# Low parts of 32 up-projection tiles made in the merge stage, stored and loaded back; dots moved out of the last stage

## The reference

```python
g_conv = jax.nn.sigmoid(g_conv + b_merge[:D_MODEL])
g_attn = jax.nn.sigmoid(g_attn + b_merge[D_MODEL:])
merged = g_conv * y_conv + g_attn * y_attn
return jnp.einsum("bsd,de->bse", merged, w_o)
...
e = (jnp.take_along_axis(i1, ci // P_TOPK, axis=-1) * N_KEYS
     + jnp.take_along_axis(i2, ci % P_TOPK, axis=-1))
g = jax.nn.softmax(vals, axis=-1)
...
a = jnp.einsum('cd,ckd->ck', xc, expert_u[ec])
w = (gc * jax.nn.gelu(a.astype(jnp.float32))).astype(x.dtype)
return jnp.einsum('ck,ckd->cd', w, expert_v[ec])
```

## Time and profile before

| | us |
|---|---|
| median of 3 runs | 2193.1 (2191.36 to 2194.11) |
| the profiled execution | 2191.2 |
| its span, first to last instruction | 2189.5 |
| TensorE busy | 2124.8 (97%) |
| VectorE busy | 1650.1 (75%) |
| ScalarE busy | 1042.0 (48%) |
| GpSimd busy | 638.7 (29%) |

### The profile page before, as it was taken

How to read it: one execution, slowest core, us unless ns; L and a number is a source line. 1 busy time by engine, 2 the same in 40 slices (tenths; PEclk the granted TensorE clock), 3 DMA queues, 4 the chain that set the end, 5 groups by cost and what they waited for, 6 DMA issues and landing times.

```text
span 2189.5 us, 33425 instructions
## 1 busy us (share of the span) xinstructions
PE 2124.8 (97%) x11713; PEld 1787.7 (82%) x11713; DVE 1650.1 (75%) x3228; ACT 1042.0 (48%) x1940; POOL 638.7 (29%) x425
## 2 busy tenths in 40 slices
PE   7999999999999988899999989999999999999999
PEld 6888888888888545687899988999998888888777
DVE  6555555534367687564399999999988989999999
ACT  5333333322243477744455535999844333343332
POOL 0000000000040000020100223777626767777773
PEclk9999999999999999999999999999999999999999
DMA  5322222232234200022355888999989999999997
GB/s 195 97 86 86 86 86 95 80 99 98 98 101 177 77 1 1 1 68 87 125 177 177 279 260 290 382 408 400 392 306 408 419 418 418 418 418 418 411 418 290
DMA packets 137228, 484.57 MB, mean 221 GB/s; under 512 B 15056, under 2 KB 30416, under 8 KB 135184
## 3 DMA queue, kind: packets, MB, share of 16 engines
q1 hardware_dynamic: 75456, 229.93, 30.0%
q0 software_dynamic: 59056, 225.14, 26.1%
q10 hardware_dynamic: 2592, 27.85, 3.1%
HBM read 435.42 MB, written 46.92 MB: 220 GB/s over the span
## 4 chain that ended last, share of the span: by engine, by line
PE 63%; DVE 21%; DMA 10%; ACT 3%; issue 2%; POOL 1%; ACTq 0%; DVEq 0%; POOLq 0%
PE bank L495 15%; PE bank L496 15%; PE bank L497 15%; DMA rows<-peer_v,idxU 9%; PE bank L1257 7%; DVE rows L2327 6%; DVE wlo L482 4%; PE bank L510 2%; DVE own L2332 2%; DVE hot L2485 2%; DVE hot L2483 2%; PE bank L610 1%; PE bank L570 1%; PE bank L813 1%; PE bank L1211 1%
## 5 line engine op out<-in xcount | busy, mean ns | idle before, releaser
L495 PE MATMUL bank<-act_hi,whi 128*128 128x320 f32 (+1 forms) x1840 | 646.4, 351 | 23.2 <-DVE wlo L482 19.8
L496 PE MATMUL bank<-act_lo,whi 128*128 128x320 f32 (+1 forms) x1840 | 635.1, 345 | 0.0
L497 PE MATMUL bank<-act_hi,wlo 128*128 128x320 f32 (+1 forms) x1840 | 634.8, 345 | 0.0
L482 DVE TENSOR_TENSOR wlo<-raw,whi 128x1024 fp32r<-128x1024 f32 x398 | 485.8, 1222 | 141.5 <-ACT whi L478 139.3
L478 ACT ACTIVATE whi<-raw 128x1024 fp32r<-128x1024 f32 x398 | 416.4, 1055 | 262.5 <-PE bank L1257 114.1
L495 PEld LDWEIGHTS bank<-act_hi,whi 128*128 128x128 f32 x1840 | 346.0, 188 | 65.7 <-DVE wlo L482 23.4
L497 PEld LDWEIGHTS bank<-act_hi,wlo 128*128 128x128 f32 x1840 | 345.8, 188 | 32.7
L496 PEld LDWEIGHTS bank<-act_lo,whi 128*128 128x128 f32 x1840 | 346.2, 188 | 31.4 <-issue 0.7
L762 POOL DMA_INDIRECT rows<-peer_u,idxU x128 | 196.7, 1537 | 337.5 <-DVE udot L2327 168.9
L1257 PE MATMUL bank<-whi,h_hi 128*128 128x512 f32 x768 | 238.4, 391 | 7.1 <-DVE wlo L482 4.2
L1257 PE MATMUL bank<-whi,h_lo 128*128 128x512 f32 x768 | 237.4, 390 | 0.0
(11 more groups left out here) (403 smaller groups left out, 2905.6 us busy)
## 6 DMA issues: line engine op xcount, KB each, us to landing
raw<-tiles SPq DMA_DIRECT2D x398, 512.0 KB, 4.9
gates_dram<-stage ACTq DMA_DIRECT2D x12, 2048.0 KB, 11.6
wg<-gates_dram POOLq DMA_DIRECT2D x16, 1536.0 KB, 17.0
acts_dram<-gelu SPq DMA_DIRECT2D x120, 160.0 KB, 5.1
hf<-acts_dram POOLq DMA_DIRECT2D x30, 640.0 KB, 13.6
bias<-alibi POOLq DMA_DIRECT2D x16, 256.0 KB, 2.9
w1s<-cmp_w POOLq DMA_DIRECT2D x1, 4096.0 KB, 13.0
res<-x_t ACTq DMA_DIRECT2D x4, 512.0 KB, 6.9
```

The costliest lines, as they stand in the source:

```text
L482: dve.tensor_tensor(wlo[:, j.slot, :], raw[:, j.slot, :], whi[:, j.slot, :].bitcast(F32), ALU.subtract).then_inc(lo_made, 1)
L495: pe.matmul(to, wh, x, start=(kc == 0), stop=False)
L496: pe.matmul(to, wh, xl, start=False, stop=False)
L497: last = pe.matmul(to, wl, x, start=False, stop=(kc == KC - 1))
```

## The change

Between the merge stage's pairs of jobs stand pairs of tiles of the up projection (jobs 36 to 67): they are loaded, rounded and split like every tile, but not multiplied; the low part is stored to a new DRAM tensor `lo_dram`. The merge stage so has 64 ring positions instead of 32, of which TensorE uses 32. VectorE hands the stored slots on (`low_stored`) when both stores of a pair have landed. In the up projection the same 32 tiles are loaded again (their high part is made again), and their low part is loaded from `lo_dram` by SyncE; VectorE only signals that it is there. The dots are redistributed: 12 for 6 in tile 2, 28 for 18 in tile 3, 72 for 76 in the gates stage, 18 for 12 in the rest, so that 62 instead of 80 stay for the last stage. Two semaphores are merged into one (`res_step`).

```diff
-J_C = J_B + 32
+J_C = J_B + 64
+EARLY_LO = range(36, 68)
-DOTS_TILE = [(0, 0), (0, 0), (6, 10), (18, 0)]
-DOTS_GATES = 76
-DOTS_REST = 12
+DOTS_TILE = [(0, 0), (0, 0), (12, 10), (28, 0)]
+DOTS_GATES = 72
+DOTS_REST = 18
@@ SyncE
+            with sp.Fori(0, J_C // RING - J_B // RING) as i:
+                for m in range(RING):
+                    load(Job(J_B + RING + m, i))
+                    if m >= 2:
+                        sp.dma_start(lo_dram[bass.ds(i * 2 + m - 2, 1), :, :],
+                                     wlo[:, m, :].bitcast(F32)).then_inc(S("lo_moved"), 16)
...
+            def store_and_load(i, at_, with_lo):
                 for m in range(RING):
-                    j = Job(J_U + m, i)
+                    j = Job(J_U + at_ + m, i)
                     was_taken(sp, j)
-                    sp.dma_start(acts_dram[bass.ds(i * RING + m, 1), :, :], gelu[:, m, :])\
+                    sp.dma_start(acts_dram[bass.ds(i * RING + at_ + m, 1), :, :], gelu[:, m, :])\
                         .then_inc(acts_stored[m], 16)
-                    load(Job(J_U + 8 + m, i))
+                    if with_lo:
+                        sp.wait_ge(S("lo_moved"), (i * RING + len(EARLY_LO) + m) * 16)
+                        sp.dma_start(wlo[:, j.slot, :].bitcast(F32), lo_dram[bass.ds(i * RING + m, 1), :, :])\
+                            .then_inc(S("lo_moved"), 16)
+                    load(Job(J_U + at_ + 8 + m, i))
+
+            first, end = EARLY_LO.start - RING, EARLY_LO.stop - RING
+            for low, high in ((0, first), (first, end), (end, U_REST)):
+                with sp.Fori(0, (high - low) // RING) as i:
+                    store_and_load(i, low, low == first)
@@ TensorE, merge stage
             with pe.Fori(0, 4) as i:
-                for m in range(8):
-                    ...
-                    multiply(pe, Job(J_B + m, i, 8), hi, lo)
+                for m in range(16):
+                    j = Job(J_B + m, i, 16)
+                    if m % 4 < 2:
+                        ...
+                        multiply(pe, j, hi, lo, after_stored(Job(J_B - 1 + m, i, 16)) if m % 4 == 0 else None)
@@ VectorE, merge stage
+                def low_stored(unit, *stored_jobs):
+                    dve.wait_ge(S("lo_moved"), (unit + 1) * 32)
+                    for j in stored_jobs:
+                        dve.wait_ge(taken[j.slot], j.turn + 1)
+                        dve.sem_inc(taken[j.slot], 1)
+                        dve.sem_inc(job_done, 1)
                 for h in range(2):
                     chunk = bass.ds(i * 2 + h, 1)
-                    make_lo(dve, J(4 * h).ahead())
-                    by_root(tg[:, :], J(4 * h), r_one[:, :])
-                    make_lo(dve, J(4 * h + 1).ahead())
+                    make_lo(dve, J(8 * h + 2))
+                    make_lo(dve, J(8 * h + 3))
+                    by_root(tg[:, :], J(8 * h), r_one[:, :])
+                    make_lo(dve, J(8 * h + 4))
                     dve.wait_ge(conv_tanh, i * 2 + h + (KC + 1))
-                    result_of(dve, J(4 * h + 1))
+                    result_of(dve, J(8 * h + 1))
                     dve.wait_ge(mg_split, i * 2 + h + 1)
                     dve.scalar_tensor_tensor(out=m1[:, :], in0=tg[:, :], scalar=1.0, in1=bank[1][:, :],
                                              op0=ALU.add, op1=ALU.mult).then_inc(taken[1], 1)
-                    make_lo(dve, J(4 * h + 2).ahead())
-                    was_taken(dve, J(4 * h + 1))
-                    by_root(tg[:, :], J(4 * h + 2), r_one[:, :])
-                    make_lo(dve, J(4 * h + 3).ahead())
+                    low_stored(i * 4 + 2 * h, J(8 * h + 2), J(8 * h + 3))
+                    make_lo(dve, J(8 * h + 5))
+                    was_taken(dve, J(8 * h + 1))
+                    make_lo(dve, J(8 * h + 6))
+                    make_lo(dve, J(8 * h + 7))
+                    by_root(tg[:, :], J(8 * h + 4), r_one[:, :])
+                    make_lo(dve, J(8 * h + 8))
                     dve.wait_ge(attn_tanh, i * 2 + h + (KC + 1))
...
+                    low_stored(i * 4 + 2 * h + 1, J(8 * h + 6), J(8 * h + 7))
+                    make_lo(dve, J(8 * h + 9))
+                    was_taken(dve, J(8 * h + 5))
@@ VectorE, up projection
             def u_job(n):
-                make_lo(dve, Job(J_U + n).ahead())
+                j = Job(J_U + n).ahead()
+                if n + AHEAD in EARLY_LO:
+                    dve.wait_ge(hi_made, j.n + 1)
+                    dve.wait_ge(S("lo_moved"), 16 * (len(EARLY_LO) + n + AHEAD - EARLY_LO.start + 1))
+                    dve.sem_inc(lo_made, 1)
+                else:
+                    make_lo(dve, j)
```

More of the change, by code:

```diff
@@ L656, in _ @@
                 load(Job(m))
-            with sp.Fori(1, (J_U + 8) // RING) as i:
+            with sp.Fori(1, J_B // RING + 1) as i:
                 for m in range(RING):
                     load(Job(m, i))
+            with sp.Fori(0, J_C // RING - J_B // RING) as i:
[4 more added lines that the diff above has]
+                                     wlo[:, m, :].bitcast(F32)).then_inc(S("lo_moved"), 16)
+            with sp.Fori(0, (J_U + 8) // RING - J_C // RING - 1) as i:
+                for m in range(RING):
+                    load(Job(J_C + RING + m, i))
             for m in range((J_U + 8) // RING * RING, J_U + 8):
                 load(Job(m))
-            with sp.Fori(0, U_REST // RING) as i:
+            def store_and_load(i, at_, with_lo):
                 for m in range(RING):
-                    j = Job(J_U + m, i)
+                    j = Job(J_U + at_ + m, i)
                     was_taken(sp, j)
-                    sp.dma_start(acts_dram[bass.ds(i * RING + m, 1), :, :], gelu[:, m, :])\
+                    sp.dma_start(acts_dram[bass.ds(i * RING + at_ + m, 1), :, :], gelu[:, m, :])\
                         .then_inc(acts_stored[m], 16)
-                    load(Job(J_U + 8 + m, i))
+                    if with_lo:
[7 more added lines that the diff above has]
+                    store_and_load(i, low, low == first)
             with sp.Fori(0, (JOBS - J_U - U_REST - 8) // RING) as i:
@@ L887, in _, with after_stored, wait, first_of_c @@
                 two_heads(c)
-            with pe.Fori(0, 4) as i:
-                for m in range(8):
-                    if m == 1:
-                        pe.wait_ge(y_split, 2 * KC)
-                    hi, lo = ((act_hi, act_lo), (yc_hi, yc_lo), (act_hi, act_lo), (ya_hi, ya_lo))[m % 4]
-                    multiply(pe, Job(J_B + m, i, 8), hi, lo)
+            def after_stored(j):
+                def wait(kc):
+                    if kc == KC - 1:
+                        result_of(pe, j)
+                return wait
+            with pe.Fori(0, 4) as i:
+                for m in range(16):
+                    j = Job(J_B + m, i, 16)
+                    if m % 4 < 2:
+                        if m == 1:
+                            pe.wait_ge(y_split, 2 * KC)
+                        hi, lo = ((act_hi, act_lo), (yc_hi, yc_lo), (act_hi, act_lo), (ya_hi, ya_lo))[m // 4 % 2 * 2 + m % 4]
+                        multiply(pe, j, hi, lo, after_stored(Job(J_B - 1 + m, i, 16)) if m % 4 == 0 else None)
+            def first_of_c(kc):
+                pe.wait_ge(mg_split, kc + 2)
+                if kc == KC - 1:
+                    result_of(pe, Job(J_C - 1))
             for m in range(8):
-                multiply(pe, Job(J_C + m), mg_hi, mg_lo,
-                         (lambda kc: pe.wait_ge(mg_split, kc + 2)) if m == 0 else None)
+                multiply(pe, Job(J_C + m), mg_hi, mg_lo, first_of_c if m == 0 else None)
             def first_of_d(kc):
@@ L1346, in J @@
                 def J(m):
-                    return Job(J_B + m, i, 8)
+                    return Job(J_B + m, i, 16)
                 for h in range(2):
-                    make_hi(act, J(4 * h).ahead())
-                    make_hi(act, J(4 * h + 1).ahead())
-                    was_taken(act, J(4 * h))
+                    make_hi(act, J(8 * h + 2))
+                    make_hi(act, J(8 * h + 3))
+                    was_taken(act, J(8 * h))
                     act.activation(tg[:, :], tg[:, :], ACT.Tanh, scale=0.5,
                                    bias=half_b[:, bass.ds(i * 2 + h, 1)]).then_inc(conv_tanh, 1)
-                    make_hi(act, J(4 * h + 2).ahead())
-                    make_hi(act, J(4 * h + 3).ahead())
-                    was_taken(act, J(4 * h + 2))
+                    for m in range(4, 8):
+                        make_hi(act, J(8 * h + m))
+                    was_taken(act, J(8 * h + 4))
                     act.activation(tg[:, :], tg[:, :], ACT.Tanh, scale=0.5,
                                    bias=half_b[:, bass.ds(i * 2 + h + 8, 1)]).then_inc(attn_tanh, 1)
+                    make_hi(act, J(8 * h + 8))
+                    make_hi(act, J(8 * h + 9))
                     act.wait_ge(merged, i * 2 + h + 1)
@@ L2572, in lay_out @@
```

(5 more changed lines are left out.)

23 lines of the change are left out of this document (11 added, 12 removed).

## The result

The changed kernel takes 2320.9 us (median of 4 runs, 2317.9 to 2329.2) where the kernel before takes 2193.6 beside it: a ratio of 1.059, interval 1.0577 to 1.0602. It is 127 us slower; 2292 was forecast, and the range reached to 2325. The profiled execution is the slowest of the four, 2329.2 us with a span of 2327.5, so its shifts add up to 138 us and not to 127. Which stage took the 11 us more in it is not known.

What follows compares the result with a forecast made beforehand. TensorE, busy 97% of the span, was taken as the bound. Span 2189.5 + 99 (routing) + 7 (merge) - 4 (gates) + 1.5 (rest) - 4.5 (last) = 2288.5; with 1.7 and 1.9, 2292 us; range 2245 to 2325.

Steps and rivals of the forecast that it cites:

- The new wait: Routing stage: the sync queue stands until each low part lands, one under way, period 6.9 us; +99 us with three more dots.
- each landing in 5 to 6: Sign in the profile after: loads of low parts on the sync queue, some 6.9 us apart, each landing in 5 to 6 us.
- the short chain: Rival, routing stage: low parts land like single loads, 3.5 to 3.8 us, period 5.0, about +38, 2231 us; 8 in 100.
- TensorE's holes: Sign, routing stage: a TensorE hole of about 3.4 us before each of jobs 37 to 67, released by VectorE or the transfer.
- the long chain: Rival, routing stage: gathers stretch landings to 6.3 to 7 us, period 7.7 and more, +124, 2317 us; 10 in 100.
- The relief: Last stage: 18 fewer dots free VectorE and DMA engines, -4.5 us; gates stage: 72 dots for 76, -4 us.
- The merge stage: Added stores make VectorE wait for landings, 22.6 us per half against TensorE's 21.7: +7 us, bounds 0 and +14.
- all landed at t + 6.3: Merge stage: four 512 KB transfers at 405 GB/s plus fixed 2.1 us land 6.3 us after the second stored low part ends.
- My bound of +14: Merge stage: upper bound of its added time, for stores landing half a microsecond slower.
- The rest of the up projection: 18 dots for 12, 6.9 us more VectorE work, mostly into idle time: +1.5 us, bounds 0 and +5.
- the relief wins: Rival: low parts arrive at least every 3.9 us, hiding the chain; kernel faster, near 2179 us; 6 in 100.

Runs made afterwards that it cites:

- the kernel that waits late: The whole change, with VectorE's wait for the stores' landing moved to just before the next write to those slots: 2287.9 us, ratio 1.043.

## Why the prediction was right, and which term was wrong

**The new wait: right, in mechanism and size.** Each step stood: the raw load waits at the line of `load`, the low part before it must land first, one is under way at a time. The period was worked out as 6.9 us and is 6.92. It was made up as 5.5 for the landing and 1.4 around it; the landings' mean is 5.4 and the rest 1.5. The pair of raw loads 1.14 us apart was the right row for the mean. The spread was not foreseen: "each landing in 5 to 6" holds for nine of the 32. Nor is the term the same in every execution: it is 97.1 us in that of the kernel that waits late and 94.2 with the old dots. A landing of 3.5 us, the short chain, didn't come. The rule of the Trainium skill for one transfer ("DMA: Bandwidth & Descriptors", section "Anatomy of one DMA — SWDGE (gpsimd) path", 2 us and the bytes at 436 GB/s) gives an estimated 3.2 us a landing and so 4.6 us a period, 74 us less over the 32. The section states it for transfers that GpSimd issues, which the prediction didn't say; these are SyncE's. The trace of the changed kernel disagrees with it: no low part lands in under 4.2 us, and the median is 5.1.

**TensorE's holes: there, but smaller than foreseen.** A hole of 3.4 us was named before each of the jobs 37 to 67; there are 28 of 2.5 us in the mean. The period is the same, so TensorE's jobs took longer: the matmuls of the jobs 36 to 71 keep it busy 167.5 us instead of 134.2, at a granted clock of 0.86 instead of 1.00. The prediction had this only in the rival of the long chain. VectorE's busy share is 47% there (106 of 225 us) where some 55 were named.

**The relief: there, and worth little.** The last stage gave 5.1 us for 22 us of VectorE and 23 us of the DMA engines, as TensorE covers the rest (its 4.2 us of waits for low parts there are gone); the gates stage 4.6. Both within 1 us of the forecast.

**The merge stage: the mechanism right, the size off by 35 us.** The step was named: VectorE waits for the landing before it makes the next needed low part. The term that was mis-sized is "all landed at t + 6.3": it is t + 7.8 and t + 8.4, because the four transfers behind one another go at about 310 GB/s and not at 405, and before the second pair a fifth stands, one more raw load, issued at 551 and overlooked. These 1.5 and 2.1 us, eight times each, are 29 of the 35 us. 4 more are the step from the landing to VectorE's next low part, 0.4 to 0.5 us and not 0.2; the last 2 lie behind the merge stage, as told at the ledger. VectorE's chain was already 0.9 us over TensorE's pace, so every added tenth went straight to the end. My bound of +14 (it should read +15: eight times 1.9) allowed for half a microsecond per landing; nearly two were needed. A rate taken from the last stage, where SyncE's loads run beside GpSimd's transfers and gathers, isn't that of a group of four on one queue.

**The rest of the up projection: +5.5 where +1.5 was taken**, the bound being +5. The kernel with the moved dots alone shows the same 5.6. 4.3 of them are one wait of TensorE in front of the last stage's first job, before and after:

```profile
PE bank L1257 <- issue: 2.7, 1, 2.7
...
PE bank L1289 <- issue: 7.0, 1, 7.0
```

Every kernel with 18 dots there has these 4.3 us and none with 12 has them, so the six dots don't all go into idle time. That they stand in front of the first gated products is read from VectorE's order; the trace names no releaser. The other 1.2 us arise at job 113, in two of the kernels with 12 dots too, and are open.

**The rival "the relief wins"** named a landing of 2.5 us as the point from which it decides. It misses a second condition, which the kernel with three low parts under way shows: even without the chain the 62 MB of the jobs 32 to 67 keep the DMA engines full for longer than TensorE needs. The low parts of these tiles double the traffic of their weights, and the dots moved there bring their gathers along.

**The range** held the time (2245 to 2325, 2320.9) near its upper end, and that is luck: the room was made for the long chain, but the chain had the forecast's period, and the merge stage's error filled the gap. One of the four executions, at 2329.2, lies above the range.

## What to carry to other kernels

When a transfer replaces a computation, look at who waits for it on the queue that issues it: a load that is released by the previous transfer turns a ring of four slots into one transfer at a time, and then the landing, not the bandwidth, is the period. Where an engine waits for a store only to reuse a buffer, put the wait in front of the reuse, not in front of other work: here that move alone was worth 33 us. And price a landing with the transfers that stand before it on the same queue, at the rate that such a group shows, and count how many times the error enters.

## What the runs showed of the hardware

- A 512 KB store of SBUF to DRAM between raw loads landed in 5.0 to 8.3 us, where a lone 512 KB load lands in 3.4; stores of half the bytes landed in 4.2 to 6.3.
- TensorE's granted clock fell with its holes: 0.86 in the mean of 1250 to 1475 us, with TensorE busy 155 of 225 us, and 0.97 in the merge stage. Below 1 means stretches at 1.2 GHz instead of 2.4. What that cost by itself no run separates; the period of the chain was the one worked out without it.
